# Stick-breaking attention in a long fp32 kernel: queries moved to the partitions, with a backward scan over sigmoids in place of triangular matmuls over logarithms

## What is computed

```python
z = einsum("qd,kd->qk", q, k) / 8              # strictly causal: key s < query t
log_not = where(mask, log_sigmoid(-z), 0)
suffix  = cumsum(log_not, axis=keys, reverse=True) - log_not
weights = where(mask, exp(log_sigmoid(z) + suffix), 0)
o = weights @ v                                # A[t,s] = sig(z_ts) * prod_{s<j<t} (1 - sig(z_tj))
o = o * rsqrt(mean(o * o, axis=-1) + 1e-6) * attn_out_g   # per head
```

## Time and profile before

| | |
|---|---|
| runs | 4690.79, 4692.12, 4679.6 us; median 4690.79 |
| span of the profiled execution | 4687.3 us |
| its mean granted TensorE clock | 0.948 |
| TensorE busy (weight loads apart) | 4199.8 us, 90% of the span |
| VectorE, ScalarE, GpSimd busy | 2113.7, 951.8, 331.2 us |
| `attention_1` | 275.4 to 698.3 us of the span |

### The profile page before, as it was taken

The page is one execution under the profiler, slowest core; times in us unless marked ns, Lnnn a source line. Parts: engine busy times, 40 slices in busy tenths (PEclk is TensorE's granted clock), DMA queues, the critical chain, the costliest instruction groups (busy, mean ns, idle before and its releaser), DMA issues. The chain is left out here.

```text
span 4687.3 us, 43781 instructions
## 1 busy us (share of the span) xinstructions
PE 4199.8 (90%) x17579; PEld 3004.8 (64%) x17579; DVE 2113.7 (45%) x2833; ACT 951.8 (20%) x1880; POOL 331.2 (7%) x257
## 2 busy tenths in 40 slices
PE   4899998999999879967779999979798969989997
PEld 3743336788887658756668888867565456359446
DVE  5112226444345565978564444462253042234834
ACT  1035551000001241142130000030143110122101
POOL 0024310000000001423000000000100000000010
PEclk9999999999999889988889999989899989989999
DMA  2111111111111111020011110121200101100121
GB/s 87 36 69 60 66 69 36 36 38 51 54 49 50 63 57 54 18 77 1 19 66 42 54 54 36 62 109 36 77 1 28 54 2 50 41 1 1 38 71 59
DMA packets 96188, 219.08 MB, mean 47 GB/s; under 512 B 9552, under 2 KB 11684, under 8 KB 96036
## 3 DMA queue, kind: packets, MB, share of 16 engines
q1 hardware_dynamic: 96036, 216.98, 12.9%
HBM read 196.00 MB, written 20.97 MB: 46 GB/s over the span
## 5 line engine op out<-in xcount | busy, mean ns | idle before, releaser
L129 PE MATMUL banks<-region_parts 128*128 128x512 f32 x3392 | 1346.0, 397 | 164.2 <-DVE weight_chunks_parts L123 125.3
L129 PEld LDWEIGHTS banks<-region_parts 128*128 128x128 f32 x3392 | 643.4, 190 | 308.3 <-DVE weight_chunks_parts L123 91.2
L130 PE MATMUL banks<-weight_chunks_parts,region_parts 128*128 128x512 f32 x1856 | 727.2, 392 | 0.0
L131 PE MATMUL banks<-region_parts 128*128 128x512 f32 x1856 | 727.1, 392 | 0.0
L131 PE MATMUL banks<-region_parts,weight_chunks_parts 128*128 128x512 f32 x1728 | 679.3, 393 | 0.0
L130 PE MATMUL banks<-region_parts 128*128 128x512 f32 x1536 | 602.6, 392 | 0.0
L130 PEld LDWEIGHTS banks<-weight_chunks_parts,region_parts 128*128 128x128 f32 x1856 | 351.7, 189 | 76.5 <-issue 4.6
L131 PEld LDWEIGHTS banks<-region_parts 128*128 128x128 f32 x1856 | 351.2, 189 | 74.3
L131 PEld LDWEIGHTS banks<-region_parts,weight_chunks_parts 128*128 128x128 f32 x1728 | 329.1, 190 | 69.6
L96 PE MATMUL banks<-region,weight_chunks 128*128 128x512 f32 (+1 forms) x832 | 346.5, 577 | 1.5 <-ACT region L1932 1.5
L901 ACT ACTIVATE region<-gain_offset 128x512 f32<-128x512 f32 x128 | 81.0, 633 | 1267.1 <-DVE gain_offset L849 1267.1
(11 more groups left out here) (301 smaller groups left out, 4805.5 us busy)
## 6 DMA issues: line engine op xcount, KB each, us to landing
weight_chunks<-in_w_in SPq DMA_DIRECT2D x22, 2048.0 KB, 8.0
weight_chunks<-in_w_up SPq DMA_DIRECT2D x16, 2048.0 KB, 8.3
weight_chunks<-in_w_down SPq DMA_DIRECT2D x16, 2048.0 KB, 7.8
weight_chunks<-in_w_ada SPq DMA_DIRECT2D x12, 2048.0 KB, 8.3
weight_chunks<-in_w_out SPq DMA_DIRECT2D x8, 2048.0 KB, 7.8
x_spill<-region SPq DMA_DIRECT2D x24, 512.0 KB, 11.7
region<-x_spill SPq DMA_DIRECT2D x24, 512.0 KB, 7.2
region<-in_x SPq DMA_DIRECT2D x8, 512.0 KB, 9.1
```

Of the source, the lines that this page charges most:

```text
L129: pe.matmul(out, m.parts(lhs[0]), m.parts(rhs[0]), start=first, stop=False)
L130: pe.matmul(out, m.parts(lhs[0]), m.parts(rhs[1]), start=False, stop=False)
L131: return pe.matmul(out, m.parts(lhs[1]), m.parts(rhs[0]), start=False, stop=last)
```

## The change

Queries go to the partitions. The work is cut into 96 parts: per pair, half, query tile t of 128 and head, the keys in chunks of at most 512, the chunk at the diagonal first. The scores become two sigmoids, of -z (`keep`) and of z (`hit`). A VectorE scan runs backwards along the row over `keep` and leaves the product of all later (1 - sigmoid); weights are `hit` times the product one place on. Each 128x128 tile of weights is transposed on TensorE, copied by ScalarE from PSUM, and multiplied with v. The modulation now has the `w_ada` tile as weights (128x128) and silu(c) as the one streamed column, four products an item, whose result is in columns at once. The head means are kept in q's place and the Ln and Exp of all pairs come at the end, over 1024 columns a pair. The pooling products move into the last parts, and GpSimd runs its pooling steps at once. The Sigmoid table is used, and the joint table of Exp and Ln isn't preloaded. A tile of 16 KB a partition (`extra`) is added, and the scratch for dynamic DMAs is set to 256 bytes. The core of the diff, new side:

```diff
...
+    groups = [(pair, half) for pair in range(N_HEADS // 2) for half in range(2)]
+    units = [(gi, t, odd) for gi, (_, half) in enumerate(groups) for t in range(4 * half, 4 * half + 4) for odd in range(2)]
+    parts = [(n, c) for n, (gi, t, _) in enumerate(units) for c in range(t // 4, -1, -1)]
+    POOLED_AT = NP - 9
 # tensor
+            def scores(i):
+                if x >= 3:
+                    pe.wait_ge(s.z_free, x - 2)
+                pe.matmul(m.bank[:, x % 3, 0:w], q[b:b + 64, pair, t * P:(t + 1) * P],
+                          k[b:b + 64, pair, c * HALF:c * HALF + w], start=True, stop=True).then_inc(s.z_done, 1)
+            def modulation(i):
...
+                for j in range(4):
+                    mm = pe.matmul(m.bank[:, 3, 4 * c + j:4 * c + j + 1], m.wbuf[:, wt.used % 2, k8, j * P:(j + 1) * P],
+                                   m.c_act[:, k8:k8 + 1], start=(k8 == 0 and j == 0), stop=(k8 == NK - 1 and j == 3),
+                                   skip_group_check=True)
+            def turn(i):
+                pe.wait_ge(s.weights, i + 1)
+                if i >= 2:
+                    pe.wait_ge(s.copied, i - 1)
+                for j in range(w // P):
+                    mm = pe.transpose(m.bank[:, 4 + i % 2, j * P:(j + 1) * P], hit[n % 3][:, lo + j * P:lo + (j + 1) * P], m.ident)
+            def values(i):
+                pe.wait_ge(s.copied, i + 1)
+                for j in range(w // P):
+                    mm = pe.matmul(m.bank[b:b + 64, 6, (t % 4) * P:(t % 4 + 1) * P], v[:, 4 * c + j, h * 64:(h + 1) * 64],
+                                   aT[i % 3][:, j * P:(j + 1) * P], start=(top and j == 0), stop=(c == 0 and j == w // P - 1),
+                                   skip_group_check=True)
+            for i in range(NP + 4):
+                if i < NP:
+                    scores(i)
+                    if ("pooled", i - POOLED_AT) in at_item:
+                        pooled(i - POOLED_AT)
+                    modulation(i)
+                if 2 <= i < NP + 2:
+                    turn(i - 2)
+                if i >= 4:
+                    values(i - 4)
...
 # scalar
-            act.preload_act_table_set(EXP_LN)
+                act.activation(keep[n % 3][:, lo:lo + w], z, ACT.Sigmoid, scale=-1.0)
+                ins = act.activation(hit[n % 3][:, lo:lo + w], z, ACT.Sigmoid)
...
+            def copy(i):
+                act.wait_ge(s.turned, i + 1)
...
+                act.activation(aT[i % 3][:, 0:w], m.bank[:, 4 + i % 2, 0:w], ACT.Copy).then_inc(s.copied, 1)
+            for i in range(NP + 3):
+                if i < NP:
+                    sigmoids(i)
...
+                if i >= 2 and i - 2 < NP:
+                    copy(i - 2)
...
+            for pair in range(4):
+                act.wait_ge(s.ss_kept, 2 * pair + 2)
+                m.act_link(act, act.activation(q[:, pair, :], q[:, pair, :], ACT.Ln, bias=m.eps_col(RMS_EPS)))
+                act.activation(q[:, pair, :], q[:, pair, :], ACT.Exp, scale=-0.5).then_inc(s.rs_ready, 1)
 # vector
+                dve.wait_ge(s.both_ready, i + 1)
+                x = reversed_(kb[:, lo:lo + w])
+                dve.tensor_tensor_scan(x, x, zeros.broadcast_to([P, w]), kb[:, lo + w:lo + w + 1],
+                                       ALU.mult, ALU.add).then_inc(s.scanned, 1)
+                dve.wait_ge(s.scanned, i + 1)
+                dve.tensor_tensor(hb[:, lo:lo + w], hb[:, lo:lo + w], kb[:, lo + 1:lo + w + 1], ALU.mult).then_inc(s.weights, 1)
+            for i in range(NP):
+                if i + 1 < NP:
+                    cap(i + 1)
+                weights(i)
+                if kept < len(groups) and i >= last_part[kept] + 9:
+                    keep_sums(kept)
...
+            for pair in range(4):
+                dve.wait_ge(s.rs_ready, pair + 1)
+                dve.scalar_tensor_tensor(o, o, m.c("attn_out_g", pair), q[:, pair, :], op0=ALU.mult, op1=ALU.mult)
...
 # gpsimd
+            for step in pool_steps(m, a, pool, u, pool_a, pool_b, s.diff_ready):
+                step()
 # build, kernel
+        m.extra = sb("extra", 4 * S)
+    nc = _bacc.Bacc("TRN2", target_bir_lowering=False, num_devices=1, dynamic_dma_scratch_size=256)
```

More of the change, by code:

```diff
@@ new lines, in attention_1 @@
+    NP = len(parts)
+    last_part = {}
+    for i, (n, c) in enumerate(parts):
+        last_part[units[n][0]] = i
+    POOLED_AT = NP - 9
+    items = []
+    for i in range(NP):
+        items.append(("scores", i))
+        if i >= POOLED_AT and i < POOLED_AT + 8:
+            items.append(("pooled", i - POOLED_AT))
+    at_item = {x: n for n, x in enumerate(items)}
+    T = m.R[1][:].rearrange("p a b -> p (a b)")
+    keep = [T[:, b * 1025:(b + 1) * 1025] for b in range(3)]
+    hit = [T[:, 3 * 1025 + b * S:3 * 1025 + (b + 1) * S] for b in range(3)]
@@ L410, in attention_1 @@
+    n_top = [sum(where(j)[7] for j in range(i + 1)) for i in range(NP)]
     with nc.Block() as block:
@@ new lines, in sigmoids @@
+            def sigmoids(i):
+                n, c, gi, t, odd, w, lo, top = where(i)
+                x = at_item["scores", i]
+                z = m.bank[:, x % 3, 0:w]
+                if top:
+                    act.wait_ge(s.capped, n_top[i])
+                else:
+                    act.wait_ge(s.z_done, x + 1)
+                if top and n >= 3:
+                    done = max(j for j in range(NP) if parts[j][0] == n - 3)
+                    act.wait_ge(s.turned, done + 1)
+                    act.wait_ge(s.weights, done + 1)
+                act.activation(keep[n % 3][:, lo:lo + w], z, ACT.Sigmoid, scale=-1.0)
+                ins = act.activation(hit[n % 3][:, lo:lo + w], z, ACT.Sigmoid)
+                ins.then_inc(s.z_free, 1)
+                act.wait_ge(s.z_free, x + 1)
+                act.sem_inc(s.both_ready, 1)
@@ new lines, in keep_sums @@
+            def keep_sums(gi):
+                pair, half = groups[gi]
+                dve.wait_ge(s.ss_done, gi + 1)
+                dve.tensor_copy(q[:, pair, half * HALF:(half + 1) * HALF], m.bank[:, 7, :]).then_inc(s.ss_kept, 1)
+            kept = 0
+            cap(0)
+            for i in range(NP):
+                if i + 1 < NP:
[3 more added lines that the diff above has]
+                    keep_sums(kept)
+                    kept += 1
@@ L2560, in build @@
         m.cst = sb("constants", 7, P)
-        m.ident, m.ones, m.negtri, m.before, m.cap, m.headmean, m.negones = (m.cst[:, t, :] for t in range(7))
+        m.ident, m.ones, m.cap, m.headmean = (m.cst[:, t, :] for t in (0, 1, 4, 5))
+        m.extra = sb("extra", 4 * S)
         m.poolfix = sb("pool_fix", 4, 16)
```

342 lines of the change are left out of this document (106 added, 236 removed).

## The result

| | before | after |
|---|---|---|
| runs, median (lowest to highest) | 4685.45 (4679.6 to 4692.12), 4 runs | 4740.25 (4728.18 to 4754.88), 4 runs |
| span of the profiled execution | 4687.3 us | 4749.0 us |
| mean granted clock | 0.948 | 0.916 |
| TensorE, VectorE, ScalarE busy | 4199.8, 2113.7, 951.8 us | 4232.4, 2195.7, 894.5 us |
| `attention_1`: last value products end / stage ends | 687.4 / 698.3 | 735.4 / 758.1 |

The changed kernel takes 1.0113 times as long, interval [1.0094, 1.0131], and its median is 54.8 us higher, where 4714 against 4690.8 was forecast, 23 us more. The median before is 4685.45 here and 4690.79 above, since a fourth run, of 4680.12, is counted. The profiled execution of the changed kernel is one of its two longer ones (4750.8 us). Of the 61.7 us between the two spans, 59.8 are in the changed stage.

A forecast was written before the change was run, and what follows sets the result against it. TensorE's own instructions were taken to bound the loop, its clock deciding: start 282.1 + loop 415 + tail 24 = 721 us against 698.3, 23 later, so 4714 us on the 4690.8 median; range 4610 to 4768.

The forecast's parts named there:

- the low share: Part of the loop's wall time at half clock: 0.58, expected at the narrow first steps of each of four head pairs.
- faster: Outcome of a whole time below 4677 us, with the loop under 378 us, a low share under 0.43; chance 0.37.
- TensorE sets the loop: In the changed stage's loop, TensorE's own instructions set the time; the other engines were costed at nothing.
- VectorE's chain: Loop's chain through VectorE's scan, costed at nothing; as a rival, it becomes the wait, 48 us more, 4762, chance 0.02.
- Loop at the high level, 301 us: TensorE's loop at full clock: 286 us for 96 steps and 288 tiles, plus 15 for head-mean and pooling products.
- thinner than any of these: Claim that the new TensorE stream, with one-column products and 64-row scores, is thinner than earlier streams with low clock.
- Waits costed at nothing: In the loop, hand-overs between TensorE and the other engines were to add 0 us.
- the chain of a step: Scores to product in one full step: 5.4 us, covered since transposes come about 8.9 us after the scores began.
- The tail, 24 us: After the last value products: head mean, Ln and Exp for four pairs, eight table loads (10.3 us), last scaling.
- The scans: VectorE's backward scans in the loop: 2.1 ns a column, 1.20 us at 512 columns, 90 us in all, hidden.
- The rival that the clock rises once and holds: Loop low for 28 us, then high: 314 us, whole time 4613 us; chance 0.25.
- The rival that it never rises: Loop at half clock throughout: 573 us, whole time 4871 us; chance 0.06.

The follow-up runs named there:

- experiment 3: Changed kernel with score products over the 128 rows of both heads of a pair instead of 64; 4647.6 us, ratio 0.9917 to the kernel before.
- experiment 7: Changed kernel with only the last of each chunk's eight modulation items computed, nothing in their place; 4618.77 us, ratio 0.9845 to the kernel before.
- experiment 1: Changed kernel with modulation streamed again (silu(c) as one weight column, 512 columns streamed), rows turned after the loop; 4643.37 us, ratio 0.9905 to the kernel before.
- experiment 4: Changed kernel with an added 128-row score product before each score product, then overwritten; 4736.28 us, ratio 1.0104 to the kernel before.
- experiment 2: Kernel before with only its modulation items changed to four one-column products, no column turning; 4678.43 us, ratio 0.9979 to the kernel before.

## Why the prediction came out as it did

The direction and the mechanism were right, a loop set by TensorE whose clock decides; 4740 is 26 us over the forecast of 4714 and within its range. In the profiled executions the miss is larger, 59.8 us in the stage against 23. That the number came so near is in part luck: no row gave the low share, which alone decided between faster and slower, and faster had a chance of 0.37.

- **TensorE sets the loop**: right. 442 of 453 us busy; transposes waited for nothing. VectorE's chain is off the path, as costed. (The 684 that the prediction has for the end of the old loop is 687.4 by the trace; no sum of the new time uses it.)
- **Loop at the high level, 301 us**: near. With the measured distances it is 96 x (0.21 + 0.91 + 0.12 + 0.14) + 288 x (0.21 + 0.11 + 0.22) + 15 = 303. Two terms were off and cancel: the fixed part of a score product is 0.21, not 0.11: in the earlier trace rows transposes follow the scores, here a modulation item does, and experiment 3 has the extra 0.1 gone once the scores have 128 rows; the modulation item is 0.91, not the 0.98 of the earlier trace rows, within its bounds of 0.86 and 1.12. At the low level the item is 1.73 (489.65 to 491.38), not 1.96, and the loop 565, not 573.
- **The low share, 0.58 of the wall time**: this is the step that failed, in size. It was 0.68. With it, 1/(0.32/303 + 0.68/565) = 443, and the loop's own waits, 10.6 us, make it 453. The reason given for the share was wrong too: it was to fall in the narrow steps and recover in the wide ones. It fell alike in both. That picture fits the kernel of experiment 7, where the modulation is nearly gone; with the modulation in, even steps of four tiles did not hold the high level for long: it is low through all of 465.7 to 540.8. The part on how thin the stream is ("thinner than any of these") was the right one, and experiments 1 and 3 show it in two ways: the same loop is at 0.93 with the modulation streamed and at 0.81 with 128 rows of scores.
- **Waits costed at nothing**: 10.6 us were missed. At each change of half pair the value products wait for ScalarE's square and copy of the one bank that they all use. The forecast checked the chain of a step, not the one of a half pair.
- **The tail, 24 us**: right, 22.7, with eight loads of 1.28 as assumed; one load instead gives 9.4 back (forecast 9). The activation starts right behind its load, 736.50 + 1.28 and 737.80. The Trainium skill's page "ScalarE: Activation LUTs", section "What ACT_TABLE_LOAD costs", counts a further drain of 1.38 us with each switch. By it the tail would have been about 34 us, an estimate from the measured 22.7 and eight such drains; no such drain shows in this trace.
- **The scans**: 1.28 us at 512 columns from 322 us on, where 1.20 was taken; 105 us in all, not 90, off the path. Before 322, while GpSimd runs its pooling steps, they took far longer: 2.23 us at 512 columns and 2.27 at 256, which takes 0.74 later. No price was put on that. That GpSimd is the cause is not shown by a run of its own. It cost nothing in the changed kernel, whose transposes waited for nothing, but in experiment 1 the long row-copy gap lies there.
- **The rival that the clock rises once and holds** did not come, but it is what experiment 1 nearly is, at 0.93 (its forecast was 4613, experiment 1 has 4643). **The rival that it never rises**: the Trainium skill's page "TensorE: Matmul & The Clock Gate", part "PE-mode transpose", says that transposes do not engage the full clock. Experiment 1 speaks against it as the cause: all 288 transposes are in its loop, which holds 1.00 from 474.5 to 553.

## What to carry to other kernels

Count a TensorE stream not only in instructions and columns but in how much of the array they fill: eight one-column passes (0.91 us) or a 64-row product (1.05) take about as long as a full product (0.95 to 0.96), but a loop with many of them can run at half clock, here for two thirds of its time, while it shows as 98% busy. If the granted clock falls in a busy stretch, change the form of the thinnest item first (stream the wide operand, fill the rows), even where that form costs as much or more in itself. And when a filler item hides a chain, price the chain before the filler is moved.

## What the runs showed of the hardware that was not expected

- **Added work cost no time.** 96 dense products worth 80 us at the high level left the loop at 441 us, where it has 432 to 453 without them (experiment 4).
- **What stands beside the thin products decides.** One-column products and 64-row scores in one unit with two wide products of 128 rows lost nothing after the first rise (1.00 for 364.3 us, experiment 2). Without these two, the 64-row scores beside streamed modulation had 0.93, beside one-column modulation 310 of 453 us low.
- **64-row products can cost about 0.1 us more, and so can the one-column item behind them**: scores of 512 columns take 1.05 us at 64 rows and 0.96 at 128, the modulation behind them 0.91 and 0.81. Which neighbour brings it isn't settled: in the earlier trace rows, where transposes follow, two such 64-row scores take 0.955 each, the pooling product behind 64-row scores takes no more than 0.96 (703.02 to 703.98), and the four value products ahead of the scores take 1.03 in either kernel.
- **A backward scan costs what a forward one does**: 1093 and 1110 ns in the mean of 96, and 1276 ns at 512 columns in both from 322 us on.
- **VectorE's scans took 1.8 to 3 times as long in the stretch in which GpSimd works**: at 256 columns 2.27 us before 322, with GpSimd busy for 34.8 of the first 36 us, and 0.74 after it. No run separates the two.
